# Output projection in another chunk order with re-read weights, and the post-norm gain applied by TensorE

## The chip, the cores and the metric

The kernel runs on one core of a Trainium2 chip. The metric is the device time of one execution in microseconds, the median of several runs. The engines of the core work side by side, each through its own list of instructions in order, and wait for one another on semaphores: TensorE (PE, with its weight loads shown apart as PEld), VectorE (DVE), ScalarE (ACT), GpSimd (POOL) and the queue of SyncE (SP), which issues nearly all DMAs. On-chip data lies in SBUF; TensorE writes into PSUM, which has eight banks here.

## What is computed

One layer of a hybrid decoder for 1,024 prompt tokens and 8 sample tokens, in float32 (D = 1024, D_FF = 2816). The part that the change touches, from the reference:

```python
mix = jnp.concatenate([ret_out, conv_out], axis=-1) @ w_out
h = h + rms_norm(mix, n_mix_post)
xf = rms_norm(h, n_ffn_pre)
gate, up = jnp.split(xf @ w_ffn_in, [D_FF], axis=-1)
h = h + rms_norm((jax.nn.silu(gate) * up) @ w_ffn_out, n_ffn_post)
```

Ahead of it stand the input projection, the retention heads and the convolution; what they give is `ret_out` and `conv_out`.

## The kernel before

**Precision.** Each large product is made of three passes (`three_pass`, L313 to L315): both operands are split into a high part and a rest (`_hi`, `_lo`), the high part by a cast on ScalarE and the rest by a subtraction, mostly on VectorE.

**Output projection.** `mix` has 1,032 rows (tokens), kept transposed in `mix_hi` and `mix_lo`. `out_job(i)` makes 128 output columns for one chunk of tokens, 24 matmuls each. There are 24 jobs: two turns of four weight slots (`w_hi`, `w_lo`), and three chunks of 344 tokens (`OUT_CHUNKS`). Turn 0 takes all three chunks (jobs 0 to 11), then the second four weight blocks come into the slots, and turn 1 takes the three chunks again (jobs 12 to 23). ScalarE copies each result from PSUM to `mixT` (`wo_evac`, L779). A token tile of 128 is whole only once turn 1 has done its chunk.

**Middle part.** Per tile `t` of 128 tokens (nine, the last with the 8 samples): `mix_back` turns the tile back into token rows by eight transposes (L1774); ScalarE sums the squares (`mix_sum`, L873); VectorE and GpSimd make the scale (`mix_var` L1271, `power` L483); `mix_scale` on VectorE writes `m_sc` = mix x scale x gain (L1279); GpSimd adds it to the residual in `h_ring` (L601); the same again for the second norm (`h_sum`, `h_var`, `h_power`, `h_scale` L1294); `h_back` transposes the result (L1784); `x_own` and `x_own_lo` split it (L902 to L906, L1306 to L1318). The feed-forward part uses sums of blocks of its input and its weights, so that seven products replace eight: `x_sums_14` on GpSimd (L555, L557), `x_sums_hi` on ScalarE (L914, L916), `x_sums_lo` on VectorE (L1328) for the input, `w_sums` on GpSimd for the weights. The list `MIX_JOBS` says how many jobs of turn 1 stand before each `mix_back` in TensorE's list, and `MIX_PRODUCTS` where the first seven products, numbered -7 to -1, stand. These use tokens of tiles 0 to 3 only. Products 0 to 6 are the same for the other tokens, product 7 is the first for all.

**Feed-forward.** Eleven groups `g`, each with 14 products and then 24 jobs `j` of the down projection (344 tokens, six matmuls each), which go round four PSUM banks. VectorE adds each result to `ffn_acc` (L1455) and makes the rests of the weight operands (`w_op_lo`, L1334); the first three operands of the next group are made within the down projection, operand 0 ahead of the first addition, operands 1 and 2 behind the additions `j` = 3 and 7.

**Order.** Each engine's list is written by hand. The SP queue loads the second four blocks of the output weights behind the write-out of `R` (L392); a slot of `raw` can be refilled once VectorE has used it.

## Time and profile before

| | us |
|---|---|
| median of 3 runs | 1263.68 (1263.42 to 1264.02) |
| the profiled execution | 1263.2 |
| its span | 1261.4 |
| TensorE busy | 1188.6 (94%) |
| VectorE busy | 747.9 (59%) |
| GpSimd busy | 424.2 (34%) |
| ScalarE busy | 415.1 (33%) |

The page of the profile gives the busy share of each engine, the span in 40 equal slices (31.5 us each) with a digit for tenths, and the clock granted to TensorE in tenths of full speed. A timeline lists instructions in order with start, length and, in brackets, the idle time ahead of them and who ended it. A matmul's record is longer than the distance from one to the next, since they are pipelined; so work on TensorE is counted from start to start.

### The profile page before, as it was taken

The numbers are of one execution on the slowest core, as the hardware profiler recorded it, in microseconds if no ns is written. First come the engines' busy times: TensorE is split into PE (matmuls) and PEld (weight loads), VectorE is DVE, ScalarE is ACT, GpSimd is POOL, SyncE is SP. The second block draws the span as 40 slices with busy tenths as digits, with TensorE's granted clock in tenths as the row PEclk, the third lists the DMA queues.
The fourth block names the chain that finished last, engine by engine and source line by source line (L and its number), as shares of the span: only waits on it lengthen the run. The fifth ranks groups of instructions, "written<-read, shape, count | busy, mean of one in ns | idle before, by whom it ended". The sixth has DMA issues, their size and how long they took to land.

```text
span 1261.4 us, 21869 instructions
## 1 busy us (share of the span) xinstructions
PE 1188.6 (94%) x8418; PEld 1165.9 (92%) x8418; DVE 747.9 (59%) x1204; ACT 415.1 (33%) x732; POOL 424.2 (34%) x304
## 2 busy tenths in 40 slices
PE   4999999999999996689999999999999999999995
PEld 3899999999899996589999999999999999999995
DVE  5349898934444216876555555555656555655657
ACT  5354444232244226541313232323232322222222
POOL 3056788231022027742222222222222222222216
PEclk8999999999979998789999999999999999999998
DMA  9211111120042214012121212121212121212143
GB/s 305 60 51 50 35 50 51 34 70 1 1 134 76 84 60 158 36 51 68 37 65 33 67 33 67 33 67 33 67 33 67 33 67 33 67 33 67 34 166 137
DMA packets 98484, 82.35 MB, mean 65 GB/s; under 512 B 2570, under 2 KB 89226, under 8 KB 98426
## 3 DMA queue, kind: packets, MB, share of 16 engines
q1 hardware_dynamic: 98098, 80.52, 20.7%
q10 hardware_dynamic: 336, 1.15, 0.2%
q8 instruction: 34, 0.56, 0.2%
q14 instruction: 16, 0.13, 0.0%
HBM read 70.76 MB, written 11.37 MB: 65 GB/s over the span
## 4 chain that ended last, share of the span: by engine, by line
PE 58%; issue 19%; POOL 13%; DVE 4%; DMA 3%; ACT 2%; POOLq 0%; ACTq 0%; DVEq 0%; SPq 0%
PE ps L313 17%; PE ps L315 17%; PE ps L314 17%; POOL act_lo L589 3%; DMA f_raw<-in_w_ffn_in 3%; POOL f_sum L573 2%; POOL f_sum L575 2%; POOL h_ring L601 1%; POOL o_last L633 1%; DVE w_ring L1334 1%; ACT w_ring L925 1%; POOL f_raw L576 1%; POOL f_raw L581 1%; DVE x_lo L1328 1%; PE ps L1668 1%
## 5 line engine op out<-in xcount | busy, mean ns | idle before, releaser
L313 PE MATMUL ps<-x_hi,w_ring 128*128 128x256 f32 (+1 forms) x1232 | 351.0, 285 | 7.3 <-DVE w_ring L1334 5.5
L315 PE MATMUL ps<-x_lo,w_ring 128*128 128x256 f32 (+1 forms) x1232 | 349.4, 284 | 0.0
L314 PE MATMUL ps<-x_hi,w_ring 128*128 128x256 f32 (+1 forms) x1232 | 348.8, 283 | 0.0
L313 PEld LDWEIGHTS ps<-x_hi,w_ring 128*128 128x128 f32 x1232 | 234.3, 190 | 8.3 <-DVE w_ring L1334 7.1
L314 PEld LDWEIGHTS ps<-x_hi,w_ring 128*128 128x128 f32 x1232 | 235.1, 191 | 0.0
L315 PEld LDWEIGHTS ps<-x_lo,w_ring 128*128 128x128 f32 x1232 | 234.3, 190 | 0.0
L313 PE MATMUL ps<-xn_hi,w_hi 128*128 128x350 f32 (+1 forms) x576 | 187.6, 326 | 0.0
L315 PE MATMUL ps<-xn_lo,w_hi 128*128 128x350 f32 (+1 forms) x576 | 185.8, 323 | 0.0
L314 PE MATMUL ps<-xn_hi,w_lo 128*128 128x350 f32 (+1 forms) x576 | 185.6, 322 | 0.0
L313 PE MATMUL ps<-act_hi,fx_hi 128*128 128x344 f32 x528 | 171.0, 324 | 7.0 <-DVE ffn_acc L1455 6.2
L314 PE MATMUL ps<-act_hi,fx_lo 128*128 128x344 f32 x528 | 168.8, 320 | 0.0
L315 PE MATMUL ps<-act_lo,fx_hi 128*128 128x344 f32 x528 | 168.1, 318 | 0.0
L1334 DVE TENSOR_TENSOR w_ring<-f_raw,w_ring 128x512 fp32r<-128x512 f32 x115 | 93.4, 814 | 110.0 <-ACT w_ring L925 108.0
L1455 DVE TENSOR_TENSOR ffn_acc<-ps,ffn_acc 128x344 f32<-128x344 f32 x240 | 117.7, 511 | 61.0 <-PE ps L315 60.7
L589 POOL TENSOR_TENSOR act_lo<-e_s,act_hi 128x516 fp32r<-128x516 f32 x44 | 60.8, 1382 | 221.0 <-ACT act_hi L944 221.0
L573 POOL TENSOR_TENSOR f_sum<-f_raw 128x512 f32<-128x512 f32 x22 | 33.8, 1534 | 268.9 <-DMA f_raw<-in_w_ffn_in 268.9
L925 ACT CAST w_ring<-f_raw 128x512 fp32r<-128x512 f32 x115 | 71.4, 622 | 127.1 <-PE ps L315 99.7
L1060 DVE SCALAR_TENSOR_TENSOR ps<-u,cw,ps 128x1024 f32<-128x1024 f32 x87 | 111.9, 1286 | 1.9
L313 PEld LDWEIGHTS ps<-act_hi,fx_hi 128*128 128x128 f32 x528 | 99.2, 188 | 12.7 <-DVE ffn_acc L1455 11.4
L315 PEld LDWEIGHTS ps<-xn_lo,w_hi 128*128 128x128 f32 x576 | 108.7, 189 | 0.0
L313 PEld LDWEIGHTS ps<-xn_hi,w_hi 128*128 128x128 f32 x576 | 108.5, 188 | 0.1
L314 PEld LDWEIGHTS ps<-xn_hi,w_lo 128*128 128x128 f32 x576 | 108.4, 188 | 0.0
(193 smaller groups left out, 1910.5 us busy)
## 6 DMA issues: line engine op xcount, KB each, us to landing
f_raw<-in_w_ffn_in SPq DMA_DIRECT2D x44, 512.0 KB, 4.3
raw<-in_w_in SPq DMA_DIRECT2D x24, 512.0 KB, 3.7
f_raw<-in_w_ffn_out SPq DMA_DIRECT2D x22, 512.0 KB, 3.2
raw<-in_w_out SPq DMA_DIRECT2D x8, 512.0 KB, 5.8
h_ring<-in_x_prompt SPq DMA_DIRECT2D x8, 512.0 KB, 4.8
h_scratch<-h_ring SPq DMA_DIRECT2D x8, 512.0 KB, 2.8
h_fin<-h_scratch SPq DMA_DIRECT2D x8, 512.0 KB
out<-o_last SPq DMA_DIRECT2D x8, 512.0 KB
```

The source lines that it names most:

```text
L313: nc.tensor.matmul(out, hi, mhi, start=first, stop=False, skip_group_check=resumes)
L314: nc.tensor.matmul(out, lo, mhi, start=False, stop=False, skip_group_check=resumes)
L315: return nc.tensor.matmul(out, hi, mlo, start=False, stop=last, skip_group_check=resumes)
L573: g.tensor_tensor(t3, f_raw[:, up, half:D], f_raw[:, up, 0:half], ALU.subtract).then_inc(s_T, 1)
L575: g.tensor_tensor(t2, t3, f_raw[:, gate, 0:half], ALU.add).then_inc(s_T, 1)
L576: g.tensor_tensor(f_raw[:, up, 0:half], f_raw[:, up, 0:half], f_raw[:, gate, 0:half], ALU.subtract).then_inc(s_T, 1)
L581: g.tensor_tensor(f_raw[:, 2, 0:half] if first else f_raw[:, gate, 0:half], f_raw[:, gate, half:D], t2, ALU.subtract).then_inc(s_T, 1)
L589: g.tensor_tensor(act_lo[:, e, c], src[:, :], act_hi[:, e, c].bitcast(F32), ALU.subtract).then_inc(s_alo, 1)
L925: s.copy(w_ring[:, k % RING, 0, :], w_op(k, first)).then_inc(s_ohi, 1)
L1060: v.scalar_tensor_tensor(out=win if w == 0 else tap_acc, in0=win, scalar=cw[:, ct, w:w + 1], in1=tap_acc, op0=ALU.mult, op1=ALU.add).then_ ...
L1334: v.tensor_tensor(w_ring[:, k % RING, 1, :], w_op(k, first), w_ring[:, k % RING, 0, :].bitcast(F32), ALU.subtract).then_inc(s_olo, 1)
L1455: v.tensor_tensor(a, ps[:, 4 + j % 4, 0:n], a, ALU.add).then_inc(s_acc, 1)
```

## The change

- The jobs have chunks of 384, 384 and 264 tokens (`WO_CHUNKS`) and another order: turn 0 chunks 0 and 1 (jobs 0 to 7), turn 1 chunks 0, 1 and 2 (jobs 8 to 19), turn 0 chunk 2 (jobs 20 to 23). For the last four the first weight blocks are read again (`load_again` on SP into the place of `w_lo`; `w_again_hi` on ScalarE, `w_again_lo` on VectorE). Jobs 12 to 23 use two PSUM banks in place of four.
- The first `mix_back` stands behind job 12 in place of job 16. The tiles go in the order `MIX_ORDER`; `u` is the place in it.
- `mix_back` is only for the sum of squares. A new step `mix_gain` on TensorE makes the tile once more, by eight float32 products of `mixT` with a diagonal of the gain (`gain_dg`, filled by eight ScalarE passes). `h_new` on VectorE scales that and adds the residual in one pass; `mix_scale` and GpSimd's addition are gone.
- `x_sums_lo` is done by GpSimd, but for the last tile.
- The sums of the first group's weights go in another order and in two parts; the gate plane is loaded behind job 20 and the up plane behind job 21 and the sixth spill of `h`.
- The second weight blocks are loaded ahead of the write-out of `R`, and split between the evacuations of jobs 5 to 8.
- In the down projection operands 1 and 2 are made behind the additions `j` = 7 and 11.

```diff
-MIX_JOBS = [(12, 13, 14, 15, 16), (17,), (18, 19, 20), (21,), (22,), (23,), (), (), (), (), ()]
+WO_CHUNKS = [(0, 3 * P), (3 * P, 3 * P), (6 * P, T_OUT - 6 * P)]
+WO_ORDER = ((0, 0), (0, 1), (1, 0), (1, 1), (1, 2), (0, 2))
+MIX_ORDER = (0, 1, 2, 3, 4, 5, 8, 6, 7)
+SECONDS = (1, 3, 5, 6, 8)
...
+            def load_again(r):
+                sp.wait_ge(s_wojob, 4 * SLOTS + r + 1)
+                sp.dma_start(w_again[:, r, :].rearrange("p (k n) -> p k n", k=KT),
+                             w_out_v[:, :, r * P:(r + 1) * P]).then_inc(raw_in[r], 16)
...
+            def x_sums_lo(u):
+
+                t, i = MIX_ORDER[u], SECONDS.index(u)
+                xh, xl, xs, o = x_block(t)
+                n = 4 if t == TILES else P
+                for j, q in enumerate((12, 20)):
+                    pool.wait_ge(s_shi, 2 * i + j + 1)
+                    g.tensor_tensor(xl[:, q:q + 8, o:o + n], xs[:, q:q + 8, o:o + n],
+                                    xh[:, q:q + 8, o:o + n].bitcast(F32), ALU.subtract).then_inc(s_slo, 1)
...
-                    g.tensor_tensor(h[t % 3][0:n, :], h[t % 3][0:n, :], m_sc[0:n, :], ALU.add).then_inc(s_h, 1)
...
+            def w_again_hi(r):
+                act.wait_ge(raw_in[r], 16 * (N_IN // SLOTS + 3))
+                s.copy(w_hi[:, r, :], w_again[:, r, :]).then_inc(s_whi, 1)
...
-                v.scalar_tensor_tensor(out=m_sc[0:n, :], in0=ps2[0:n, 1, :],
-                                       scalar=st[0:n, 114 + t:115 + t], in1=gain_mp[0:n, :],
-                                       op0=ALU.mult, op1=ALU.mult).then_inc(s_mg, 1)
+                hh = h[u % 3][0:n, :]
+                v.scalar_tensor_tensor(out=hh, in0=ps2[0:n, 2 if u < 6 else 1, :], scalar=st[0:n, 114 + t:115 + t], in1=hh,
+                                       op0=ALU.mult, op1=ALU.add).then_inc(s_h, 1)
...
-                    if j in (3, 7) and not last:
-                        w_op_lo(g + 1, 1 + j // 4)
+                    if j in (7, 11) and not last:
+                        w_op_lo(g + 1, 1 + j // 8)
...
+            def mix_gain(u):
+                c0, n = OUT_TILES[MIX_ORDER[u]]
+                pe.wait_ge(s_diag, KT)
+                if u >= 6:
+                    pe.wait_ge(s_mss, u + 1)
+                elif u >= 1:
+                    pe.wait_ge(s_h, u)
+                for k in range(KT):
+                    ins = mm(ps2[0:n, 2 if u < 6 else 1, k * P:(k + 1) * P], mixT[:, k, c0:c0 + n], gain_dg[:, k, :],
+                             start=True, stop=True)
+                ins.then_inc(s_mT, 1)
...
+            for uu, jobs in enumerate(((12,), (13,), (14,), (15, 16), (17, 18), (19, 20))):
+                for i in jobs:
                     out_job(i)
...
+                mix_back(uu)
+                mix_gain(uu)
+                if uu >= 2:
+                    h_back(uu - 2)
+            out_job(21)
+            h_back(4)
+            out_job(22)
+            out_job(23)
+            mix_back(6)
+            product(0, -7, True)
+            mix_gain(6)
+            h_back(5)
+            mix_back(7)
+            product(0, -6, True)
```

**ScalarE's list ahead of job 20's weights.** L779 (before) and L841 (now) copy a job's result, L873 and L946 are a sum of squares, L902 to L916 and L978 to L992 split the input of the feed-forward part, L940 is `w_again_hi`. Before, where the copies of jobs 22 and 23 stand:

```order
L779 COPY mixT<-ps 128x344 [waits out_job_done,kv_done]
L873 ACTIVATE x_junk,st<-ps 128x8x128 [waits h_sumsq,mix_transposed]
L873 ACTIVATE x_junk,st<-h_ring_73 128x8x128 [waits mix_sumsq,h_done]
L902 COPY x_a<-ps 128x1024 [waits x_sums_1_4,x_sums_3_2,h_transposed]
L903 CAST x_hi<-ps 128x8x128
L914 CAST x_hi<-x_sum 128x8x128 [waits x_sums_3_2]
L916 CAST x_hi<-x_sum 128x8x128 [waits x_sums_1_4]
L779 COPY mixT<-ps 128x344 [waits out_job_done,kv_done]
```

Now, from the copies of jobs 17 and 18 to the re-read blocks of jobs 20 to 22:

```order
L841 COPY mixT<-ps 128x264 [waits out_job_done,kv_done] x2
L946 ACTIVATE x_junk,st<-ps 128x8x128 [waits h_sumsq,mix_transposed]
L946 ACTIVATE x_junk,st<-h_ring_75 128x8x128 [waits mix_sumsq,h_done]
L978 COPY x_a<-ps 128x1024 [waits x_sums_1_4,x_sums_3_2,h_transposed]
L979 CAST x_hi<-ps 128x8x128
L990 CAST x_hi<-x_sum 128x8x128 [waits x_sums_3_2]
L992 CAST x_hi<-x_sum 128x8x128 [waits x_sums_1_4]
L940 CAST w_hi<-w_again 128x1024 [waits raw_in0]
L841 COPY mixT<-ps 128x264 [waits out_job_done,kv_done] x2
L946 ACTIVATE x_junk,st<-ps 128x8x128 [waits h_sumsq,mix_transposed]
L982 CAST x_hi<-ps 128x4x128 [waits h_transposed]
L940 CAST w_hi<-w_again 128x1024 [waits raw_in1]
```

The casts of the re-read blocks stand behind the copies that wait for `h_back` of the tile two places earlier (`h_transposed`).

**VectorE's list ahead of job 21's weights**, now (L1376 is `w_again_lo`, L1394 `h_new`, L1410 `h_scale`, L1429 to L1435 `x_own_lo` of an odd tile):

```order
L1384 TENSOR_SCALAR st<-st 128x1 [waits mix_sumsq]
L1401 TENSOR_SCALAR st<-st 128x1 [waits h_sumsq]
L1394 SCALAR_TENSOR_TENSOR h_ring_77<-ps,st,h_ring_77 128x1024 [waits h_in2,mix_transposed,mix_rstd]
L1410 SCALAR_TENSOR_TENSOR h_sc<-h_ring_76,st,gain_fp 128x1024 [waits h_transposed,h_rstd]
L1429 TENSOR_TENSOR x_sum<-x_a,ps 128x4x128 [waits h_transposed,x_first_half_copied]
L1433 TENSOR_TENSOR x_sum<-ps,x_sum 128x4x128 [waits xf_hi_done,x_sums_3_2]
L1435 TENSOR_TENSOR x_lo<-ps,x_hi 128x4x128
L1376 TENSOR_TENSOR w_lo<-w_again,w_hi 128x1024 [waits w_hi_done] x2
```

The rests of the blocks for jobs 21 and 22 stand behind five passes for tiles 3 to 5.

**GpSimd's list where the feed-forward part begins.** Before (L601 adds the residual, L573 to L581 are the weight sums, L483 a power, L555 and L557 `x_sums_14`):

```order
L601 TENSOR_TENSOR h_ring_73<-h_ring_73,m_sc 128x1024 [waits h_in0,mix_scaled]
L573 TENSOR_TENSOR f_sum<-f_raw 128x512 [waits out_job_done,ffn_raw_in1,ffn_raw_in0]
L575 TENSOR_TENSOR f_sum<-f_sum,f_raw 128x512 [waits ffn_w_sums]
L576 TENSOR_TENSOR f_raw<-f_raw 128x512
L581 TENSOR_TENSOR f_raw<-f_raw,f_sum 128x512 [waits ffn_w_sums]
L483 TENSOR_TENSOR st<-st,nhalf 128x1 [waits mix_var]
```

Now (L598 is `x_sums_lo`, L627 to L635 the weight sums, L509 a power, L586 and L588 `x_sums_14`):

```order
L598 TENSOR_TENSOR x_lo<-x_sum,x_hi 128x8x128 [waits x_sums_hi] x2
L627 TENSOR_TENSOR f_raw<-f_raw 128x512 [waits ffn_raw_in1,ffn_raw_in0]
L630 TENSOR_TENSOR f_raw<-f_raw 128x512 [waits out_job_done,ffn_w_sums]
L509 TENSOR_TENSOR st<-st,nhalf 8x1 [waits mix_var]
L586 TENSOR_TENSOR x_sum<-x_sum,x_a 128x4x128 [waits out_job_done,x_sums_3_2]
L588 TENSOR_TENSOR x_sum<-x_a,x_sum 128x4x128
L509 TENSOR_TENSOR st<-st,nhalf 8x1 [waits h_var]
L633 TENSOR_TENSOR f_raw<-f_raw 128x512 [waits ffn_w_sums]
L635 TENSOR_TENSOR f_sum<-f_raw 128x512 [waits out_job_done]
```

The additions of the residual are gone from it, `x_sums_lo` has come in, and the powers of the last tiles stand between the parts of the weight sums.

## Rows read from the trace of the kernel before

**Rows 1.** The page: TensorE in 40 slices, busy tenths and granted clock.
```profile
PE   4999999999999996689999999999999999999995
PEclk8999999999979998789999999999999999999998
```

**Rows 2.** Waits of TensorE from 430 to 660 us: total, times, longest.
```profile
PE ps L1774 <- DVE m_sc L1279: 7.7, 3, 2.7
PE ps L1784 <- DVE x_lo L1318: 7.0, 4, 3.7
PE ps L313 <- DVE w_ring L1334: 5.5, 2, 4.1
```

**Rows 3.** Timeline of TensorE: start, length, line, work, idle time ahead.
```profile
434.66 0.39 PE L313 MATMUL ps<-mix_hi,w_hi 128*128 128x344 f32 x1 [0.64 <-issue]
...
453.56 1.03 PE L1774 MATMUL ps<-t_sm,mixT 128*128 128x128 f32 x8
454.35 0.40 PE L313 MATMUL ps<-mix_hi,w_hi 128*128 128x344 f32 x1
...
491.48 1.10 PE L1774 MATMUL ps<-t_sm,mixT 128*128 128x128 f32 x8 [2.18 <-ACT mixT L779]
492.41 1.87 PE L1784 MATMUL ps<-t_sm,h_sc 128*128 128x128 f32 x8
...
540.01 0.84 PE L1784 MATMUL ps<-t_sm,h_sc 8*128 8x8 f32 x8 [3.66 <-DVE x_lo L1318]
...
558.31 0.39 PE L313 MATMUL ps<-x_hi,w_ring 128*128 128x260 f32 x1 [0.96 <-ACT e_sg L940]
```

**Rows 4.** A stretch: us, PE, PEld, DVE, ACT, POOL busy, granted clock, DMA.
```profile
500.00:510.00 10.00, 5.65 (x24) 4.50 (x23) 7.18 (x7) 5.49 (x7) 9.04 (x8) 0.50 0.45 161
```

**Rows 5.** Timeline of TensorE in the retention part: four float32 products, then transposes.
```profile
339.12 1.06 PE L1603 MATMUL ps<-qT,kT 128*128 128x128 f32 x8
340.01 0.60 PE L1614 MATMUL ps<-t_sm,kT 128*128 128x128 f32 x4
```

**Rows 6.** Timeline of ScalarE and VectorE: one pass of each kind.
```profile
489.08 1.06 ACT L914 CAST x_hi<-x_sum 128x1024 fp32r<-128x1024 f32 x1
...
456.67 1.29 DVE L1279 SCALAR_TENSOR_TENSOR m_sc<-ps,st,gain_mp 128x1024 f32<-128x1024 f32 x1 [0.66 <-POOL st L483]
...
498.44 0.69 DVE L1316 TENSOR_TENSOR x_sum<-ps,x_sum 128x512 f32<-128x512 f32 x1
```

**Rows 7.** Timeline of GpSimd: a power, `conv_lo`, the residual, a weight sum, `x_sums_14`.
```profile
396.43 2.21 POOL L525 TENSOR_TENSOR mix_lo<-u,mix_hi 128x1024 fp32r<-128x1024 f32 x1
...
456.09 0.55 POOL L483 TENSOR_TENSOR st<-st,nhalf 128x1 f32<-128x1 f32 x1 [44.25 <-DVE st L1271]
...
489.06 3.33 POOL L601 TENSOR_TENSOR h_ring<-h_ring,m_sc 128x1024 f32<-128x1024 f32 x1 [0.89 <-DVE m_sc L1279]
...
499.98 1.28 POOL L555 TENSOR_TENSOR x_sum<-x_sum,x_a 128x512 f32<-128x512 f32 x1
...
512.08 1.72 POOL L576 TENSOR_TENSOR f_raw<-f_raw 128x512 f32<-128x512 f32 x1
```

**Rows 8.** DMA issues: KB each, median us from issue to landing.
```profile
raw<-in_w_out SPq DMA_DIRECT2D x8, 512.0 KB, 5.8
```

**Rows 9.** Timeline of TensorE ahead of job 8 of the output projection.
```profile
418.71 0.40 PE L313 MATMUL ps<-mix_hi,w_hi 128*128 128x344 f32 x1 [0.85 <-DVE mix_lo L1261]
```

**Rows 10.** A group's down projection: TensorE and VectorE; last, TensorE's waits there, 640 us on.
```profile
712.62 0.32 PE L313 MATMUL ps<-act_hi,fx_hi 128*128 128x344 f32 x1
713.50 0.42 PE L313 MATMUL ps<-act_hi,fx_hi 128*128 128x344 f32 x1 [0.25 <-DVE ffn_acc L1455]
...
711.91 1.11 DVE L1334 TENSOR_TENSOR w_ring<-f_sum,w_ring 128x512 fp32r<-128x512 f32 x1 [1.49 <-ACT w_ring L925]
712.94 1.77 DVE L1455 TENSOR_TENSOR ffn_acc<-ps,ffn_acc 128x344 f32<-128x344 f32 x4
...
PE ps L313 <- DVE ffn_acc L1455: 6.2, 18, 0.4
```

More of the change, by code:

```diff
@@ L278, in w_op_ready @@
             else:
-                eng.wait_ge(s_T, 4 * i + {3: 1, 1: 2, 4: 3, 2: 4}[p])
+                eng.wait_ge(s_T, 4 * i + ({4: 1, 1: 2, 2: 3, 3: 4} if first and not e else {3: 1, 1: 2, 4: 3, 2: 4})[p])
         def w_op(k, first):
@@ L290, in w_op @@
             if p == 1:
-                return f_sum[:, 1, :]
+                return f_raw[:, 2, half:D] if first and e == 0 else f_sum[:, 1, :]
             if p == 2:
@@ L568, in w_sums @@
                 pool.wait_ge(fraw_in[up], 32 * gg + (32 if e else 16))
[L569 to L572 removed]
+                pool.wait_ge(s_olo, splits(gg, 7 * e - 4))
                 g.tensor_tensor(t3, f_raw[:, up, half:D], f_raw[:, up, 0:half], ALU.subtract).then_inc(s_T, 1)
@@ new lines, in _ @@
+            h_var(5)
+            h_scale(5)
+            x_own_lo(4)
+            w_again_lo(3)
+            w_op_lo(0, -7, True)
+            mix_var(6)
+            h_new(6)
+            x_own_lo(5)
+            h_var(6)
+            h_scale(6)
+            w_op_lo(0, -6, True)
+            mix_var(7)
+            h_new(7)
+            w_op_lo(0, -5, True)
+            product_step(0, -7, True)
+            h_var(7)
+            h_scale(7)
+            x_own_lo(6)
+            mix_var(8)
+            h_new(8)
```

470 lines of the change are left out of this document (284 added, 186 removed).

## The prediction

> **What bounds the kernel now.** I read the slices of the page first. TensorE is at nine tenths nearly everywhere; the one long hole is slices 16 to 19, some 500 to 570 us, and there its clock falls too [rows 1]. Then the waits of TensorE in that part: it waits for VectorE's `m_sc` (7.7 us), for the split of `h_back`'s result (7.0) and for weight operands (5.5) [rows 2]. So this stage is bound by the round per tile through all engines, not by TensorE. The timeline shows where it starts: jobs 12 to 16 run without a gap from 434.66 to 453.56, 3.78 us each; job 23 is done at some 489.3, since the copy of its result (VectorE and ScalarE being behind) lets the sixth `mix_back` start at 491.48 after 2.18 us of idling; the last `h_back` starts at 540.01; the second half of product 7 starts at 558.31, and from there TensorE is full again [rows 3]. From 500 to 510 us it is busy 5.65 us of 10 with 0.50 of its clock, the 1.2 GHz level [rows 4]; `h_back` takes 1.87 us there [rows 3]. What the change gives is read from when TensorE is full again (558.31 now), and from the feed-forward groups behind it.
>
> I took each engine's list in its new order and gave every step the length of its row, each starting when its engine is free and what it waits for is there (0.1 us for a handover). The same walk through the old lists, with the old clock, has the last `h_back` at 540.0, where the row says 540.01.
>
> **The jobs themselves.** All 24 jobs cover the same columns, so their sum stays. But those of 384 tokens, 0 to 15, take 3.78 x 384 / 344 = 4.2 us, and the last eight 2.9. Job 12 then starts 12 x 0.4 = 4.8 us later. Job 8 no longer needs the samples' rest, so its wait of 0.85 us goes [rows 9]; the second weight blocks are loaded early enough (5.8 us [rows 8], some 25 us ahead), so their splits are hidden behind jobs 5 to 9. Job 12 starts at about 438.6.
>
> **The gain on TensorE.** No row shows these products, but the retention part has four float32 ones of the same size: 0.89 us from start to start, eight records [rows 5]. So `mix_gain` is 1.78 us per tile, 16.0 us for nine, where eight transposes take 0.79 (453.56 to 454.35 [rows 3]). Below, the transposes' own price is the bound, 0.8 us less per tile; above I take none, since shape and type are the same. The Trainium skill ("TensorE: Matmul & The Clock Gate", Terms) has the transpose mode four times as fast for float32, which would be 3.2 us per tile and 12 us more; the rows have a factor of two, and they decide. For places 0 to 5 the 1.78 us lie on TensorE's path.
>
> **Rounds 0 to 5.** Between two `mix_back` now stand one or two jobs and 0.8 + 1.8 + 0.9 us more. Round 2 is the shortest whole one, 4.2 + 3.5 = 7.7 us. A tile's way through squares (1.2), power (0.55) and `h_new` (1.3, as `m_sc` [rows 6]) is 3.4 us with the handovers, so the waits for `m_sc` and for the splits go; GpSimd's addition of 3.33 us [rows 7] goes from the round too. Jobs 12 to 19, five rounds and three `h_back` are 28.4 + 5 x 2.57 + 3 x 0.87 = 43.9 us: TensorE could start job 20 at 482.5.
>
> **The re-read weights.** Here a wait takes the place of those removed. The loads are early: issued when jobs 16 to 19 are done, landed 5.8 us on. But ScalarE casts block 0 behind the splits of tile 2, which wait for `h_back(2)`, the step right ahead of job 19. From that moment: two copies and two casts of the sums (4 x 0.95), the cast (1.06 [rows 6]), VectorE's rest (1.2), handovers: 6.2 us, with job 19 (2.9) over it. **TensorE waits 3.3 us** for job 20. Job 21 stands behind `h_back(3)`. Once ScalarE has summed for tile 4, VectorE goes through `h_new(5)`, `h_scale(4)`, three passes of 512 (0.69 [rows 6], 0.6 apart) and the rest of block 1: 5.7 us, all behind TensorE's arrival: **5.6 us**. Block 3 waits in the same way for `h_back(4)` and its splits: **2.5 us** ahead of job 23. Queued behind are the copy of job 23 and with it all last tiles. Sum 11.4 us. The second wait follows the first closely, and in the rows 2.18 us of idling after two smaller ones ended in the half clock [rows 3, 4]; so I let job 21 run at half clock (+2.8). Job 23 is done at 512.7, where it was 489.3.
>
> The Trainium skill says in the same page ("HAM oscillation — how this bites in real kernels") that waits between bursts of matmuls make each burst begin on the slow clock. By that rule job 20 and the last two jobs would be slow as well, 3 to 6 us more; that is rival C.
>
> **The last three tiles.** They are fewer than the four that stood behind job 23 before, and TensorE is not what bounds them: product -6 is. Its operand needs the up plane (issued only behind job 21) and two of GpSimd's weight sums (1.6 each), which stand behind `x_sums_lo` of tiles 2 and 3 (2 x 2.8); and its rest stands on VectorE behind `h_scale(6)`, which waits for GpSimd's `x_sums_14` of tile 5 (2 x 1.28) and a power (0.55) [rows 7]. That puts product -6 at 528. `x_sums_lo` on GpSimd is bounded by `conv_lo` with VectorE idle, 2.21, and by the addition beside VectorE, 3.33 [rows 7]; I take 2.8, and each end moves the result by 1.8 us. The Trainium skill ("SBUF — State Buffer", Who interferes with whom) has it that a VectorE pass with two SBUF inputs shuts GpSimd's reads out. By this `h_new`, with one input in PSUM, costs GpSimd nothing and `h_scale` does; the two rows agree.
>
> From there the last two tiles: `h_back` of place 7 at 537, of place 8 at 547.5, held by a power that waits behind `x_sums_lo` of tile 5. It was 540.01, so 7.5 us later. Behind it two products (-2 and -1) stand where one stood: 1.5 more. **TensorE is full again 9 us later**, at 567.3. With the full clock all through, the same walk gives 5.
>
> **The feed-forward groups.** In ten of eleven groups VectorE makes operand 1 between the additions 3 and 4: it waits 1.49 us for ScalarE and works 1.11, and addition 4 starts at 712.94. So job 8 of the down projection starts 0.88 us after the last row ahead of it instead of 0.47, and loses some 0.1 again in its first matmul [rows 10]. There are 18 waits in the nine groups shown, two each, 6.2 us as idle time [rows 10]. The change takes away the second of each pair: addition 4 would follow at 710.4, ahead of need, and operand 1, made behind addition 7, has an addition every 0.94 us to hide in (0.52 of work). It saves 0.5 x 10 = **5.0 us**. The first of each pair stays: operand 0 is where it was. At least nothing is saved, if the wait only moves to job 12.
>
> **Sum.** +9.0 - 5.0 = +4.0 us on the profiled execution (1263.2, with a span of 1261.4), which stands 0.5 below the median. On the median of 1263.68: **1267.7**.
>
> **Rivals.**
> - A, the clock holds at 2.4 GHz through the waits for the re-read weights. For it: the waits of 3.3 and 5.6 us have 6 us of matmuls between them. Against: the row at 0.50. Then +5 - 5 = 0: 1263.7.
> - B, the change works as meant: ScalarE and VectorE are early enough and jobs 20 to 23 start without a wait, with no fall of the clock. 11.4 + 2.8 less on TensorE, of which the last three tiles give some 2 back: 1255.5. Against it is the place of the casts in ScalarE's list. It decides for B if `w_again_lo` of block 1 ends by 492.
> - B2, the products with the diagonal cost what transposes cost: the end moves by 4.6 us earlier, 1263; with GpSimd at 2.21 also, 1261.
> - C, TensorE falls to half clock at the first re-read wait and stays there until job 23, and again in the last tiles: +13 - 5, 1271.7. It decides for C if job 20 already runs on the half clock.
> - D, the waits in the down projection only move, from job 8 to job 12: +9, 1272.7. Against: the additions have 0.42 us of slack each from there on.
>
> **How the numbers follow.** Forecast (1264.5 to 1270) 0.45; A with B2 (1261 to 1264.5) 0.19; B and what lies near it 0.15; C 0.13; D 0.08. The range takes in B partly, both ends of GpSimd's price, C and D: 1256 to 1274. A measurement of this kernel can tell about 0.2%, 2.5 us, from no change: faster than 1261.2 takes B and a part of B2, 0.20; slower than 1266.2 takes the upper part of the forecast, C and D, 0.56; the rest, 0.24, is the same.
>
> **What would show it.** In the profile after: waits of TensorE for VectorE's `w_again_lo` (some 3, 6 and 2.5 us, the second the longest); no wait for `m_sc`; `mix_gain` as 16 records per tile at about 0.11 us; product -6 some 15 us behind job 23; the first full stretch of the feed-forward part from about 567; half as many waits for `ffn_acc` as before (9 where there were 18), 0.44 each. I am wrong if `w_again_lo` is early, if the diagonal's products are cheap, or if the waits for `ffn_acc` are still two per group.

## The result, and the profile after

The changed kernel takes **1274.26 us** (median of 4 runs, 1273.06 to 1275.55), the kernel before 1263.85 beside it (4 runs, 1263.42 to 1265.54): ratio 1.0080, 95% interval 1.0063 to 1.0097. It is slower by some 10 us; I had forecast 1267.7, slower by 4. The profile below is of an execution of 1275.34 us.

The page of the changed kernel, TensorE's busy tenths and granted clock [rows 1]:

```profile
span 1273.6 us, 22169 instructions
...
PE   4999999999999996679999999999999999999995
...
PEclk9999999999979998889999999999999999999998
```

The hole is still there, in slices 16 to 18. What stands in it has changed. The waits of TensorE from 400 to 640 us, then those from 640 us on (total, times, longest), against [rows 2] and the last row of [rows 10]:

```profile
PE ps L330 <- DVE w_lo L1376: 11.9, 3, 6.1
PE ps L330 <- DVE w_ring L1441: 7.6, 2, 7.3
PE ps L330 <- DVE x_lo L1526: 3.5, 1, 3.5
PE ps L330 <- DVE e_s L1451: 2.7, 1, 2.7
...
PE ps L330 <- DVE ffn_acc L1597: 4.0, 9, 0.4
```

No wait for a scaled tile is left (`m_sc`, 7.7 us; those for `h_new`, the pass in its place, are 1.4), and those of `h_back` for the splits fell from 7.0 to 1.3. In their place TensorE waits for the re-read weights (L1376, `w_again_lo`), three times, and for an operand of the feed-forward part. Of the 18 waits for `ffn_acc` 9 are left.

The timeline of TensorE in the changed kernel (start, length, line, work, idle time ahead), against [rows 3]:

```profile
380.43 0.42 PE L330 MATMUL ps<-mixa_hi,w_hi 128*128 128x384 f32 x1
...
440.37 0.44 PE L330 MATMUL ps<-mixa_hi,w_hi 128*128 128x384 f32 x1 [0.62 <-ACT mixT L841]
...
451.50 1.03 PE L1916 MATMUL ps<-t_sm,mixT 128*128 128x128 f32 x8
452.37 1.95 PE L1927 MATMUL ps<-gain_dg,mixT 128*128 128x128 f32 x16
454.07 0.42 PE L330 MATMUL ps<-mixa_hi,w_hi 128*128 128x384 f32 x1
...
488.48 0.39 PE L330 MATMUL ps<-mixb_hi,w_hi 128*128 128x264 f32 x1 [3.58 <-DVE w_lo L1376]
...
502.89 0.59 PE L330 MATMUL ps<-mixb_hi,w_hi 128*128 128x264 f32 x1 [6.15 <-DVE w_lo L1376]
...
513.91 0.59 PE L330 MATMUL ps<-mixb_hi,w_hi 128*128 128x264 f32 x1 [2.20 <-DVE w_lo L1376]
...
533.86 0.58 PE L330 MATMUL ps<-x_hi,w_ring 128*128 128x256 f32 x1 [7.35 <-DVE w_ring L1441]
...
554.25 1.07 PE L1939 MATMUL ps<-t_sm,h_sc 128*128 128x128 f32 x8 [1.26 <-DVE x_lo L1423]
...
563.16 0.56 PE L330 MATMUL ps<-x_hi,w_ring 128*128 128x260 f32 x1 [3.48 <-DVE x_lo L1526]
...
594.42 0.32 PE L330 MATMUL ps<-act_hi,fx_hi 128*128 128x344 f32 x1
```

These are jobs 0 and 12; a tile's transposes (0.87 us to the next start) and its products with the diagonal (1.70 us to the next start, 1.79 in other rounds); jobs 20, 21 and 23; product -6; the last `h_back`; the second half of a product; and the first product of the down projection. Two rows of the kernel before that answer to the first and the last of these:

```profile
378.69 0.40 PE L313 MATMUL ps<-mix_hi,w_hi 128*128 128x344 f32 x1
...
576.97 0.32 PE L313 MATMUL ps<-act_hi,fx_hi 128*128 128x344 f32 x1
```

With these rows the difference can be laid out by place. Between the two profiled executions the spans differ by 12.2 us:

| stretch | before | after | difference |
|---|---|---|---|
| start to job 0 | 378.69 | 380.43 | +1.7 |
| job 0 to job 12 | 55.97 | 59.94 | +4.0 |
| job 12 to the down projection | 142.31 | 154.05 | +11.7 |
| from there to the end | 684.4 | 679.2 | -5.2 |

The first line can't be put down to the change: in the profiles of my kernels below, whose code up to there is the changed kernel's, job 0 starts anywhere from 378.13 to 381.41. Without it the sum is 10.5, beside 10.4 by the medians. So below I measure from job 12 to the down projection (**142.3 before, 154.05 after**), and leave positions in the program out.

Busy time and clock of the changed kernel by stretches (us, then PE, PEld, DVE, ACT, POOL busy, granted clock, DMA), against [rows 4]:

```profile
480.00:490.00 10.00, 6.42 (x55) 6.21 (x54) 5.46 (x6) 6.69 (x10) 6.09 (x4) 1.00 0.51 156
490.00:500.00 10.00, 6.74 (x46) 6.50 (x44) 3.61 (x6) 5.12 (x8) 1.75 (x3) 0.83 0.32 106
500.00:510.00 10.00, 7.11 (x44) 7.12 (x45) 5.20 (x5) 1.97 (x4) 3.75 (x3) 0.66 0.07 20
510.00:520.00 10.00, 7.27 (x47) 6.61 (x45) 3.91 (x4) 5.29 (x8) 6.95 (x5) 0.83 0.26 85
...
530.00:540.00 10.00, 5.85 (x36) 5.64 (x36) 4.65 (x4) 3.40 (x5) 2.67 (x3) 0.66 0.00 0
```

Behind each of the waits some of the work runs at the 1.2 GHz level. From 500 to 510 ScalarE is busy 1.97 us of 10, GpSimd 3.75, VectorE 5.20: the engines wait for one another, and none of them is full.

Last, VectorE and GpSimd in the changed kernel at the two places that my walk had shorter, and between them (519.64, 519.73) the rest for product -7 beside a weight sum:

```profile
500.93 4.12 DVE L1376 TENSOR_TENSOR w_lo<-w_again,w_hi 128x1024 fp32r<-128x1024 f32 x2
...
501.71 2.25 POOL L588 TENSOR_TENSOR x_sum<-x_a,x_sum 128x512 f32<-128x512 f32 x1
...
519.64 0.69 DVE L1441 TENSOR_TENSOR w_ring<-f_raw,w_ring 128x512 fp32r<-128x512 f32 x1 [5.78 <-ACT w_ring L1001]
...
519.73 1.74 POOL L630 TENSOR_TENSOR f_raw<-f_raw 128x512 f32<-128x512 f32 x1
...
529.71 3.49 DVE L1410 SCALAR_TENSOR_TENSOR h_sc<-h_ring,st,gain_fp 8x1024 f32<-8x1024 f32 x1 [2.44 <-POOL st L509]
533.13 0.67 DVE L1441 TENSOR_TENSOR w_ring<-f_raw,w_ring 128x512 fp32r<-128x512 f32 x1
...
529.65 1.25 POOL L633 TENSOR_TENSOR f_raw<-f_raw 128x512 f32<-128x512 f32 x1
530.87 1.25 POOL L635 TENSOR_TENSOR f_sum<-f_raw 128x512 f32<-128x512 f32 x1
```

The rest for product -6 (533.13) stands behind `h_scale` of place 6, a pass over 8 rows that takes 3.49 us beside GpSimd's weight sums.

### The profile page after: what moved, and what is told of

It is laid out like the page before. It is cut to its first block, busy times and chain, and to the rows that moved or that the text cites. A ratio compares the mean times of both kernels' runs of the same rounds, so it can differ in the third digit from the quotient of the medians.

```text
span 1273.6 us, 22169 instructions
## 1 busy us (share of the span) xinstructions
PE 1203.7 (95%) x8562; PEld 1184.8 (93%) x8562; DVE 744.8 (58%) x1200; ACT 421.1 (33%) x744; POOL 406.5 (32%) x303
## 4 chain that ended last, share of the span: by engine, by line
PE 50%; issue 3%; DVE 2%; POOL 2%; ACT 1%; DVEq 0%; POOLq 0%; ACTq 0%
PE ps L330 17%; PE ps L332 17%; PE ps L331 16%; POOL o_last L695 1%; DVE w_ring L1441 1%; POOL st L509 1%; ACT w_ring L1001 0%; DVE e_s L1485 0%; DVE ffn_acc L1597 0%; DVE o_last L1572 0%; POOL x_sum L588 0%; POOLq L86 0%; DVE h_ring L1394 0%; POOL x_sum L586 0%; DVE h_sc L1410 0%
## 5 line engine op out<-in xcount | busy, mean ns | idle before, releaser
L330 PEld LDWEIGHTS ps<-x_hi,w_ring 128*128 128x128 f32 x1232 | 234.6, 190 | 14.7 <-DVE w_ring L1441 11.0
L1441 DVE TENSOR_TENSOR w_ring<-f_raw,w_ring 128x512 fp32r<-128x512 f32 x117 | 98.5, 843 | 115.5 <-ACT w_ring L1001 114.9
L1597 DVE TENSOR_TENSOR ffn_acc<-ps,ffn_acc 128x344 f32<-128x344 f32 x240 | 120.9, 513 | 72.5 <-PE ps L332 72.0
L509 POOL TENSOR_TENSOR st<-st,nhalf 128x1 f32<-128x1 f32 (+4 forms) x54 | 41.9, 776 | 213.7 <-DVE st L1327 78.6
L331 PEld LDWEIGHTS ps<-xn_hi,w_lo 128*128 128x128 f32 x576 | 108.9, 189 | 0.0
```

Source lines behind the costliest of these rows:

```text
L330: nc.tensor.matmul(out, hi, mhi, start=first, stop=False, skip_group_check=resumes)
L331: nc.tensor.matmul(out, lo, mhi, start=False, stop=False, skip_group_check=resumes)
L509: g.tensor_tensor(dst, src, nhalf[0:src.shape[0], 0:src.shape[1]], ALU.pow).then_inc(done, 1)
L1441: v.tensor_tensor(w_ring[:, k % RING, 1, :], w_op(k, first), w_ring[:, k % RING, 0, :].bitcast(F32), ALU.subtract).then_inc(s_olo, 1)
L1597: v.tensor_tensor(a, ps[:, 4 + j % 4, 0:n], a, ALU.add).then_inc(s_acc, 1)
```

## The experiments

All kernels against the kernel before, run in turn with it. "Less than after" is the ratio's distance from the changed kernel's 1.0080, times 1263.6; each has an uncertainty of 2.5 to 3 us, since both intervals go into it. The last column is the stretch from job 12 to the down projection in the one profiled execution. It scatters too: up to job 23 kernels 4 and 5 have the changed kernel's code, and in both the step behind job 23 (the transposes of place 6) starts 77.8 us behind job 12, where the changed kernel's trace has 78.8.

| kernel | median us | ratio, 95% | less than after | stretch |
|---|---|---|---|---|
| before | 1263.3 to 1263.9 | 1 | | 142.31 |
| changed | 1274.26 | 1.0080 (1.0063 to 1.0097) | | 154.05 |
| 1 before, operands late | 1258.25 | 0.9959 (0.9947 to 0.9971) | | 142.35 |
| 2 casts a round earlier | 1261.11 | 0.9991 (0.9980 to 1.0002) | 11.2 | 140.97 |
| 3 transposes for the gain | 1268.61 | 1.0048 (1.0030 to 1.0065) | 4.0 | 147.64 |
| 4 gain of place 7 first | 1271.39 | 1.0065 (1.0048 to 1.0082) | 1.9 | 148.09 |
| 5 operand of -6 early | 1266.96 | 1.0022 (1.0012 to 1.0032) | 7.3 | 145.72 |
| 6 both, 2 and 5 | 1254.78 | 0.9921 (0.9905 to 0.9938) | 20.1 | 135.78 |
| 7 as 6, pair 1 later | 1257.69 | 0.9944 (0.9927 to 0.9960) | 17.2 | 137.73 |
| 8 as 6, transposes | 1253.33 | 0.9903 (0.9883 to 0.9923) | 22.4 | 133.52 |
| 9 sums on VectorE | 1273.07 | 1.0066 (1.0048 to 1.0084) | 1.8 | 154.20 |
| 10 as 6, sums first | 1254.56 | 0.9922 (0.9905 to 0.9938) | 20.0 | 134.57 |
| 11 as 10, pair 5 later | 1256.00 | 0.9937 (0.9919 to 0.9955) | 18.1 | 135.37 |
| 12 waits filled | 1270.86 | 1.0055 (1.0038 to 1.0071) | 3.2 | 150.44 |

**1. One line of the change alone, in the kernel before.**

```diff
-                    if j in (3, 7) and not last:
-                        w_op_lo(g + 1, 1 + j // 4)
+                    if j in (7, 11) and not last:
+                        w_op_lo(g + 1, 1 + j // 8)
```

> The kernel before, with one line of the change alone: VectorE makes the next group's operand 2 behind addition 11 of the down projection (and operand 1 behind addition 7, where operand 1 stood behind addition 3 and operand 2 behind addition 7). My theory: this line alone carries the gain of the feed-forward groups, -5.0 us, so 1258.9 us, with 9 waits of TensorE for ffn_acc behind 640 us where there were 18, and nothing changed ahead of 600 us. Rival 1: the waits only move to a later job, 18 waits and 1263.9 us (0). Rival 2: the gain seen in the changed kernel's groups came from something else in it, then 0 here as well, but with 18 waits in their old place.

Ratio 0.9959, -5.2 us, stretch unchanged at 142.35. TensorE's waits behind 640 us (the kernel before had 18 [rows 10]):

```profile
PE ps L313 <- DVE ffn_acc L1455: 4.0, 9, 0.5
```

The theory holds and both rivals fall. This line is worth as much alone as in the changed kernel (-5.2 in the table by place), so what the other parts of the change cost is not 10 us but 15.6.

**2. The re-read weights a round earlier.**

```diff
@@ ScalarE, rounds 0 to 5
+                if uu == 3:
+                    w_again_hi(0)
                 if uu == 4:
                     x_sums_hi(1)
-                    w_again_hi(0)
-                if uu == 5:
                     w_again_hi(1)
                     w_again_hi(2)
+                if uu == 5:
+                    w_again_hi(3)
             wo_evac(21)
             h_sum(5)
             x_own(4)
-            w_again_hi(3)
@@ VectorE
-                for r in {4: (0,), 5: (1, 2)}.get(uu, ()):
+                for r in {3: (0,), 4: (1, 2), 5: (3,)}.get(uu, ()):
                     w_again_lo(r)
...
-            w_again_lo(3)
```

> The changed kernel with ScalarE's casts and VectorE's rests of the re-read weight blocks one round earlier (block 0 at the end of round 3, blocks 1 and 2 at the end of round 4, block 3 at the end of round 5); loads, products and all else as they are. Theory T1 (the re-read weights' place in the lists costs 11.9 us of waits and, by the fall of the clock behind them, some 6 us more; the last tiles follow job 23): no wait of TensorE for w_lo L1376, full clock from 490 to 515 us, job 23 done some 15 us earlier than 518.7, of which the last tiles give some 4 back: -11 us, 1263. Rival T3 (the last tiles are bound by GpSimd's and VectorE's lists and not by job 23): the waits go, and product -6 waits longer than 7.35 us in their place: -3 us, 1271. Rival T2 (TensorE's own added work, 16 us of gain products, is the loss): -5 us or less, with no wait left ahead of job 23.

Measured -11.2 us, stretch -13.1; the theory said -11. TensorE's longest waits in this kernel, and then three rows of its timeline:

```profile
PE ps L330 <- DVE w_ring L1442: 8.5, 2, 7.3
PE ps L1939 <- DVE x_lo L1436: 2.8, 1, 2.8
```

```profile
504.23 1.04 PE L1916 MATMUL ps<-t_sm,mixT 128*8 128x128 f32 x8 [0.52 <-ACT mixT L841]
...
519.89 0.58 PE L330 MATMUL ps<-x_hi,w_ring 128*128 128x256 f32 x1 [7.34 <-DVE w_ring L1442]
...
579.53 0.32 PE L330 MATMUL ps<-act_hi,fx_hi 128*128 128x344 f32 x1
```

No wait for `w_lo` is left, and the loads were early enough for it: it was the place in the lists. The transposes of place 6, the step behind job 23, come 65.7 us behind job 12 (438.56 here) instead of 78.8. The full clock did not come back everywhere: a new wait of 2.8 us for a split stands ahead of job 22, and the clock is 0.83 from 490 to 500. Rival T3 falls: product -6 waits as long as before (7.3) and comes 81.3 us behind job 12 instead of 93.5; it follows job 23 and does not take the gain back. T2 (-5 or less) falls too. The theory's own sum was right in part by luck: it had job 23 some 15 us earlier and 4 given back by the last tiles; the rows have the step behind it 13.1 earlier and, at the down projection, nothing given back.

**5. The operand of product -6 early** (4 came first, and is below).

```diff
@@ GpSimd
             first_w_sums(0)
             mix_power(6)
+            first_w_sums(1)
             x_sums_14(5)
             h_power(6)
-            first_w_sums(1)
             mix_power(7)
@@ ScalarE
             mix_sum(6)
+            w_op_hi(0, -6, True)
             x_own(5)
             h_sum(6)
-            w_op_hi(0, -6, True)
@@ VectorE
             mix_var(6)
+            w_op_lo(0, -6, True)
             h_new(6)
             x_own_lo(5)
             h_var(6)
-            h_scale(6)
-            w_op_lo(0, -6, True)
             mix_var(7)
+            h_scale(6)
```

> The changed kernel with the operand of product -6 made earlier, and nothing else: ScalarE casts it behind the squares of place 6, VectorE makes its rest ahead of h_new of place 6, GpSimd makes its last two weight sums in the hole ahead of x_sums_14 of place 5, and VectorE's mean of place 7 goes ahead of h_scale of place 6. The operand's data are there at 521.5, but its rest is made at 533.1, behind h_scale of place 6, which takes 3.49 us beside those weight sums on GpSimd. Theory: the wait of 7.35 us goes, h_scale of place 6 takes 1.3 us again, gain products of place 7 follow at once and place 8 comes 7 us earlier: -6 us, 1268. Rival A: only product -6 is earlier, the places 7 and 8 are bound by their own chain (squares, power, h_new): -2 us, 1272. Rival B: h_scale of place 6 stays at 3.5 us, since what slows it is its 8 rows and not GpSimd: then the row says so, and -5 us.

Measured -7.3 us for the -6 expected; of the stretch's -8.3, 0.9 is there already at the step behind job 23, ahead of which nothing was changed. VectorE in this kernel:

```profile
519.53 2.96 DVE L1441 TENSOR_TENSOR w_ring<-f_raw,w_ring 128x512 fp32r<-128x512 f32 x1 [0.66 <-ACT w_ring L1001]
...
528.11 1.27 DVE L1410 SCALAR_TENSOR_TENSOR h_sc<-h_ring,st,gain_fp 8x1024 f32<-8x1024 f32 x1 [1.86 <-POOL st L509]
```

The wait of 7.35 us is gone. `h_scale` of place 6 takes 1.27 us where none of GpSimd's weight sums runs beside it, on the same 8 rows: rival B falls, and rival A (-2) with it. The edit moves four things at once, so how the 7.3 us divide among them is not shown. What came instead is the rest of product -6, 2.96 us instead of 0.67, since it now runs beside the weight sums (519.45 to 521.93).

**6. Both moves.**

> The changed kernel with both moves: casts and rests of the re-read blocks one round earlier, and the operand of product -6 earlier. Nothing is left out. Theory: the two losses lie one behind the other (ahead of job 23 and behind it), so they add: -13 from the first, -6 from the second: 1255 us, and with 16 us of gain products still on TensorE it is faster than the kernel before by 8 us. Rival: the last tiles take over what the first move gave: 1261, as with the casts alone.

Measured 1254.78, -20.1 us against the changed kernel, where 11.2 + 7.3 = 18.5 was the sum of the two; the stretch is 135.78, -18.3 for 13.1 + 8.3 = 21.4. By the medians they add; the stretch falls 3 us short of the sum, in a profile of the slowest of this kernel's four runs (1257.93). This kernel computes all that the kernel before computes and beats it by 0.8% (0.9905 to 0.9938), and kernel 1, the kernel before with the one line, by 0.4%.

**3 and 8. What the products with the diagonal cost.**

```diff
-                    ins = mm(..., mixT[:, k, c0:c0 + n], gain_dg[:, k, :], start=True, stop=True)
+                    ins = tr(..., mixT[:, k, c0:c0 + n], ident)
```

Both kernels leave the gain out of the output; they serve only for its price.

> The changed kernel with the eight products with the diagonal of the gain per tile made transposes (identity in place of the diagonal), so the post-norm gain is left out of the output: 0.87 us instead of 1.79 on TensorE, all waits as they are. Theory: 6 tiles lie on TensorE's path ahead of job 20, 0.9 us each, less what ScalarE's and VectorE's chain behind h_back takes over, and tile 7's stands in the last round: -4 us, 1270. Rival T2 (the products on TensorE are the whole loss): all nine count and more than linearly, -8 us or more, 1266. Rival T3 (hidden under the waits for weights): within 1 us, 1274.

> As the kernel with both moves, and the products with the diagonal made transposes (the post-norm gain is left out of the output). It prices the gain products where no wait for re-read weights stands behind them. Theory: 0.92 us per tile on TensorE's path for places 0 to 5 (5.5) and at least one of the last three (0.9): -6 us against the kernel with both moves. Rival (hidden): within 1 us of it. Rival (more than their length, since each place's round is on the path): -8 us.

In the changed kernel -4.0 us (stretch -6.4), as expected, though the first two waits for the re-read weights grew from 3.58 and 6.15 us to 4.08 and 7.07; with both moves made only -2.3 by the ratio (intervals overlap; stretch -2.3), where I expected -6. My theory for kernel 8 was wrong. TensorE's waits in it show where most of it went:

```profile
PE ps L1916 <- DVE h_ring L1395: 4.8, 2, 3.8
PE ps L1938 <- DVE x_lo L1436: 4.6, 2, 4.3
```

In kernel 6 these two are 3.4 and 2.8: they grew by 3.2 us, and the waits for `e_s` and `e_sg` in the last rounds by 1.6. With shorter rounds the tile's way through the other engines ends last, and of the 8.3 us that nine tiles save on TensorE 2.3 reach the end. Rival T2, the products as the whole loss, is refuted by both kernels.

**4. The gain of place 7 ahead of product -6.**

```diff
-            product(0, -6, True)
             mix_gain(7)
+            product(0, -6, True)
```

> The changed kernel with TensorE's products for the gain of place 7 ahead of product -6 of the first feed-forward group, instead of behind it; nothing else. Theory: place 7's h_new starts at 539.2 only since its gain products stand behind product -6, which waits 7.35 us for its operand; ahead of it they are done by 529, and VectorE gets to h_new at 533.8, 5.4 us earlier; place 8 follows: -4 us, 1270. Rival: the last round is bound by the chain of operands for products -5 and -4, or by the half clock, not by place 7: within 1 us, 1274.

-1.9 us, with intervals that overlap the changed kernel's: it can't be told from nothing by the times. The stretch says -6.0, but a piece of it is the clock's scatter: the code up to job 23 is the changed kernel's, and yet the clock stood at 1.00 from 490 to 500, where the changed kernel's was 0.83:

```profile
490.00:500.00 10.00, 5.51 (x49) 5.27 (x47) 4.84 (x8) 5.12 (x8) 2.84 (x4) 1.00 0.32 107
```

That piece is 1.0 us (the step behind job 23 is at 77.8 instead of 78.8). The other 5 are of one execution, the fastest of this kernel's four (1269.70), so it stays open whether the move gains the 4 us; kernel 5 took the wait away in another way.

**9. The lower parts of the sums on VectorE again** (GpSimd's `x_sums_lo` taken out, the same passes in four holes of VectorE's list).

> The changed kernel with one part of the change undone: the lower parts of the sums (x_sums_lo) are made by VectorE again, as in the kernel before, in holes of its list (pair 1 behind the rest of re-read block 0, pair 3 behind that of block 3, pair 5 behind the mean of place 7, pair 6 in the last round), and not by GpSimd. Theory of the prediction (GpSimd's x_sums_lo hold up the weight sums, and with them product -6): the weight sums start at 512.2 instead of 518.4, and product -6 gains up to 6 us: -5, 1269. Rival (product -6 hangs on the place of its cast and of its rest in ScalarE's and VectorE's lists, as the kernel with that operand made early showed): the sums come early and product -6 does not; only the passes that ran slowly beside GpSimd gain (the rests of blocks 1 and 2, 4.12 us for two, and the two of 1.80 and 2.52 us): -2 us, 1272.

GpSimd's first two weight sums in this kernel, VectorE's `h_scale` of place 6, and TensorE's wait for the operand:

```profile
513.45 1.27 POOL L617 TENSOR_TENSOR f_raw<-f_raw 128x512 f32<-128x512 f32 x1 [1.78 <-DMA f_raw<-in_w_ffn_in]
514.80 2.14 POOL L620 TENSOR_TENSOR f_raw<-f_raw 128x512 f32<-128x512 f32 x1
...
532.57 3.50 DVE L1395 SCALAR_TENSOR_TENSOR h_sc<-h_ring,st,gain_fp 8x1024 f32<-8x1024 f32 x1 [2.45 <-POOL st L509]
```

```profile
PE ps L330 <- DVE w_ring L1437: 7.6, 2, 7.4
```

The sums for product -6 are there at 516.9, 75.6 us behind job 12 (441.32 here), instead of 521.5, 81.1 behind it. TensorE's wait for the operand is the same 7.4 us, product -6 comes 14.7 us behind the transposes of place 6 in both kernels, and its rest again stands behind an `h_scale` of 3.5 us. GpSimd's `x_sums_lo` was not what held product -6. The time is -1.8 us, near the rival's -2, but the intervals overlap and the stretch (154.20) is no shorter, in a profile where all of job 20 runs on the low clock: what the move is worth can't be told from nothing.

**12. The waits filled.**

```diff
@@ TensorE, ahead of the wait for the weights of job i
+                if i >= 20:
+                    pe.wait_ge(s_wo, CREDIT_AB + i - 1)
+                    for q in range((15, 27, 0, 9)[i - 20]):
+                        mm(ps[:, i % 2, 0:P], mixT[:, q % KT, 0:P], gain_dg[:, q % KT, :], start=True, stop=True)
```

> The changed kernel with idle time of TensorE filled, nothing moved: ahead of its wait for the re-read weights TensorE makes 15 (job 20), 27 (job 21) and 9 (job 23) products of 128x128 into the bank that the job writes over afterwards (their results are not used), 0.22 us each, 3.3, 5.9 and 2.0 us in waits of 3.6, 6.15 and 2.2. It parts the waits from the clock that falls with them. Theory (my forecast's second cause: the waits let the clock fall): granted clock 1.00 from 480 to 520 us, so job 20's last 12 products, job 21's 18 slow ones and job 23's 15 take 0.12 us instead of 0.22 from start to start, and mix_back of place 5 0.87 instead of 1.26: -5 us, 1269, with the time at which each job's weights are ready moved only as far. Rival: the clock falls all the same (0.83, 0.66, 0.83), or the fillers come too late: 0 to +2 us. Rival: the jobs are faster and the last tiles take it all back, since they follow GpSimd and VectorE: within 1 us.

```profile
480.00:490.00 10.00, 9.75 (x85) 9.56 (x84) 5.48 (x6) 7.48 (x11) 5.17 (x4) 1.00 0.60 184
490.00:500.00 10.00, 10.00 (x90) 10.00 (x89) 4.21 (x7) 5.12 (x8) 2.81 (x4) 1.00 0.32 107
500.00:510.00 10.00, 9.87 (x84) 9.68 (x83) 6.78 (x6) 4.42 (x7) 3.93 (x3) 1.00 0.31 90
510.00:520.00 10.00, 8.90 (x72) 7.51 (x70) 2.42 (x4) 3.95 (x7) 8.63 (x5) 1.00 0.04 17
```

The clock stays at 2.4 GHz with TensorE kept at work, and with 51 useless products more the kernel is 3.2 us faster by the medians, where the intervals still overlap (1.0038 to 1.0071, 1.0063 to 1.0097). The stretch says the same, -3.6: from job 12 to product -6 it is 88.8 us instead of 93.5, -4.7, of which 1 is given back further on. Against the traces of kernels 4 and 5 the step behind job 23 is 4.0 earlier, against the changed kernel's 4.9. This is the price of the clock behind these waits alone, with the waits as they were, and some third of the 13.1 us that kernel 2 took out of the stretch.

**7, 10 and 11. Further moves on GpSimd.** Kernel 7 puts `x_sums_lo` of pair 1 behind round 5, which is ahead of the power that `h_scale` of place 5 waits for; 10 makes the first two weight sums ahead of `x_sums_lo` of pair 3 and the operand of product -6 right behind that of -7; 11 puts `x_sums_lo` of pair 5 behind `h_scale` of place 8.

```diff
@@ 7, GpSimd, rounds 0 to 5 and behind
-                if uu - 3 in SECONDS:
-                    x_sums_lo(uu - 3)
+            x_sums_lo(1)
             h_power(5)
@@ 10, GpSimd (and ScalarE, VectorE: w_op of -6 ahead of mix_sum and mix_var of 6)
-            x_sums_lo(3)
             first_w_sums(0)
+            x_sums_lo(3)
@@ 11, GpSimd
-            x_sums_lo(5)
             h_power(8)
+            pool.wait_ge(s_hs, 9)
+            x_sums_lo(5)
```

> As the kernel with both moves, and GpSimd's x_sums_lo of tile pair 1 (5.7 us for two) placed behind the powers of round 5 instead of in round 4, where it runs beside VectorE's rests of blocks 1 and 2 (4.94 us for two, 2.5 without). Theory: the two rests take 2.5 us again, h_back of place 4 no longer waits (2.8 us), but x_sums_14 of place 3 comes 2 us later: -1.5 us against the kernel with both moves. Rival: GpSimd's list is the bound, and the delay behind it costs as much: 0 or +2.

> The kernel with both moves, and further: GpSimd makes its first two weight sums ahead of x_sums_lo of pair 3, and ScalarE's cast and VectorE's rest for product -6 go ahead of the squares and the mean of place 6. There the rest of product -6 took 2.81 us beside GpSimd's weight sums, with h_new of place 6 behind it, and the next mix_back waited 2.73 us. Theory: h_new of place 6 starts 2.3 us earlier and all behind it: -2.5 us against the kernel with both moves (1252). Rival: the last three tiles are bound further on (the chain squares, power, h_new, squares, power, h_scale of places 7 and 8 does not shorten, but it starts earlier too), so less than 1 us only if the clock falls in the longer round.

> As the kernel before it, and GpSimd's x_sums_lo of pair 5 behind h_scale of place 8 (5.15 us for two, until then behind x_sums_14 of place 6, beside VectorE's rests of 1.78 and 2.54 us and ahead of the power of place 8). Theory: those two rests take 0.7 us each, the power of place 8 does not wait, h_back of place 8 comes 3 us earlier: -2.5 us against the kernel before it. Rival: what is moved is only later in the way, of x_sums_14 of place 8 and of the second half of product 1, which waits 3.5 us already: 0 or +2.

The theory missed in all three, and the rivals came nearer. Kernel 7 is 2.9 us slower than kernel 6 by the medians (the intervals overlap; stretch +2.0). Its rows, VectorE first, then GpSimd:

```profile
487.79 2.36 DVE L1376 TENSOR_TENSOR w_lo<-w_again,w_hi 128x1024 fp32r<-128x1024 f32 x2 [1.35 <-ACT w_hi L939]
...
504.80 3.36 DVE L1410 SCALAR_TENSOR_TENSOR h_sc<-h_ring,st,gain_fp 128x1024 f32<-128x1024 f32 x1 [6.34 <-POOL st L509]
508.08 1.21 DVE L1423 TENSOR_TENSOR x_lo<-ps,x_hi 128x1024 fp32r<-128x1024 f32 x1
...
499.51 4.76 POOL L598 TENSOR_TENSOR x_lo<-x_sum,x_hi 128x1024 fp32r<-128x1024 f32 x2
504.24 0.53 POOL L509 TENSOR_TENSOR st<-st,nhalf 128x1 f32<-128x1 f32 x1
504.74 5.63 POOL L598 TENSOR_TENSOR x_lo<-x_sum,x_hi 128x1024 fp32r<-128x1024 f32 x2
```

The two rests did fall to 2.36 us. But the power at 504.24, 0.53 us of work, now stands behind 4.76 us of sums, and `h_scale` of place 5 waits 6.34 us for it. Kernel 10 took 1.2 us out of the stretch and nothing out of the median; its wait for the operand of product -7 grew from 1.2 to 2.2 us. Kernel 11 is no gain (+1.4 in the median, +0.8 in the stretch). My reading, which no run tests, is that from here several chains within a microsecond or two of each other bound the part.

## Why the forecast was right, and where it was short

The direction holds, and so does the mechanism up to job 23; the size was 6.6 us short, a loss of 10.4 us where I had 4.0. The 1274.26 us lie above my forecast's own band (1264.5 to 1270) and at the very end of the range (1256 to 1274; 1.0080 times 1263.68 is 1273.8). By my own steps, each from job 12 on where the stretch allows it:

| step | forecast | measured |
|---|---|---|
| jobs wider, 0 to 12 | +3.9 | +4.0 |
| gain per tile | 1.78 | 1.79 |
| TensorE ready for job 20, after job 12 | 43.9 | 44.5 |
| waits for the re-read weights | 3.3, 5.6, 2.5 | 3.58, 6.15, 2.20 |
| job 23 done, after job 12 | 74.1 | 78.3 |
| product -6, after job 12 | 89.4 | 93.5 |
| last `h_back`, after job 12 | 108.9 | 113.9 |
| down projection, after job 12 | 147.4 | 154.05 |
| feed-forward groups | -5.0 | -5.2 |

- **The jobs, the gain, the waits: right.** The products with the diagonal take what the four float32 products of the retention part took [rows 5], twice a transpose. I had weighed against this the factor of four that the Trainium skill gives the transpose mode ("TensorE: Matmul & The Clock Gate", Terms): the rows of the changed kernel have 1.79 to 0.87, a factor of two. The three waits add to 11.9 us for a forecast of 11.4, in the order said and for the reason said; kernel 2 shows that it is the casts' place in the lists.
- **The clock: mis-sized.** This is the step that failed first. I let job 21 alone run slowly, +2.8 us. The rows show the second half of job 20, most of job 21 and most of job 23 at 0.22 us from start to start, and the transposes behind job 20 slowed too, and kernel 12 prices all that at 4.7 us by product -6. In the trace job 20 takes 4.2 us for my 2.9, the tile's steps behind it 4.1 for 3.5, job 21 4.9 for 5.7 and job 23 4.7 for 2.9, together 2.9 us more; with the waits' 0.5 and 0.6 ahead of job 20 that is all but 0.2 of the 4.2 us by which job 23 is late. (In the traces of kernels 4 and 5 it is 1 us less late.) The rule of the Trainium skill that I had made rival C of (the same page, "HAM oscillation — how this bites in real kernels") is borne out here for jobs 21 and 23, which begin slowly behind their waits; job 20 begins at full clock behind 3.58 us and turns slow halfway. It is not borne out each time: in the traces of kernels 4 and 5, with the same waits, job 20 runs at full clock to its end and job 23 begins so, while in kernel 9's all of job 20 and of job 23 is slow. Of the surcharge of 3 to 6 us that I had worked out for it 2 to 3 came (4.7 for 2.8 by kernel 12, 2.9 more by the rows above).
- **Product -6: the right time for a wrong reason.** I had it 15.3 us behind job 23, held by GpSimd's `x_sums_lo` ahead of the weight sums. It is 15.2 behind. But with the sums 5 us earlier (kernel 9) it does not move, and with its cast and rest moved in ScalarE's and VectorE's lists (kernel 5, which also moves two weight sums and a mean) its wait goes. So this step failed as a mechanism, and that its number came out is luck. I had named `h_scale` of place 6 ahead of the rest, at some 1.3 us; it took 3.49, 2.2 more, which stands against what the sums did not cost. `x_sums_lo` itself was sized well (2.8; measured 2.6 to 2.8), and it was no matter: the term had no place in the sum. (The 2.21 us that I took as its price with VectorE idle has VectorE at work beside it, on passes with at most one SBUF input.) Here the rule of the Trainium skill that VectorE's pass with two SBUF inputs and GpSimd shut one another out ("SBUF — State Buffer", Who interferes with whom) told more than I took from it: I had used it for what GpSimd loses, and it was VectorE that lost, 3.49 us for 1.27.
- **Behind the last `h_back`: a wait that I did not have.** The second half of a product waits 3.48 us for VectorE's last sums (563.16) and the stretch from 560 to 570 has 0.66 of the clock; I put the 1.7 us by which this part was longer than in my walk down to these two; no run parts them. My walk had ended at the last `h_back` and put 1.5 us of matmuls behind it.
- **The groups: right.** Half the waits went, -5.2 for -5.0, and kernel 1 has them alone.
- **The rivals.** A (no fall of the clock) would have been right on the price of the clock, which kernel 12 has, but it did fall. B needed the casts early, and kernel 2 is B: it is 11.2 us less than the changed kernel, where B was 12.2 less than my forecast. So the price of the waits was right, and what both lack is the same. B2 is kernel 3: -4.0 for -4.6. C (half clock from the first re-read wait to job 23, and again in the last tiles; 1271.7) comes nearest in mechanism: in part of job 20, in job 21 and in job 23 the clock was low, not in job 22, and again from 530 to 540 and from 560 to 570 us (0.66). D (1272.7) is nearest in number and fell: the waits did not move to job 12.

What the parts of the change come to: the line in the feed-forward groups -5.2; the wider jobs +4.0; the stretch +11.7, where the place of four casts alone costs 13.1, that of one operand 8.3, and both together 18.3. With the lists put right the rest of the change (the new order, the gain on TensorE, the residual in VectorE's pass) is worth some 4.7 us more than the line alone (0.9922, kernel 10, against 0.9959), though it carries 16 us of products more.

## What to carry to other kernels

When a step is given new work, the question is not what that work costs its engine but where in each in-order list it stands, and behind whose wait: four casts of 1 us behind a copy that waits for TensorE cost 11 us, and one round earlier they leave no wait for their weights. After a predicted wait ask what is on TensorE behind it and price that at the low clock as well; and a short step that others wait for (a power of 0.5 us) must not be put behind long passes of its engine: in kernel 7 VectorE waited 6.3 us for one. Before comparing two profiles, measure from the first instruction that differs: here the start scattered by 3 us.
